# First feed-forward stage of a two-block transformer kernel: its first two weight chunks read the residual times the norm weight, and the root is applied to their banks

## The reference, cut to what matters

```
h = x
h = h + 0.5 * _swiglu(_rmsnorm(h, ffn1_norm[i]), ffn1_w_in[i], ffn1_w_out[i])
```

## Time and profile before

| | us |
|---|---|
| median of 3 runs | 1517.85 (1516.86 to 1518.26) |
| span of the profiled execution | 1515.1 |
| median less span | 2.75 |
| PE busy in that span | 1482.7 (98%) |
| DVE busy | 1177.7 (78%) |
| ACT busy | 819.8 (54%) |

### The profile page before, as it was taken

The page is one execution under the profiler, slowest core; times in us unless marked ns, Lnnn a source line. Parts: engine busy times, 40 slices in busy tenths (PEclk is TensorE's granted clock), DMA queues, the critical chain, the costliest instruction groups (busy, mean ns, idle before and its releaser), DMA issues.

```text
span 1515.1 us, 22326 instructions
## 1 busy us (share of the span) xinstructions
PE 1482.7 (98%) x9258; PEld 1317.9 (87%) x9258; DVE 1177.7 (78%) x1394; ACT 819.8 (54%) x998; POOL 49.6 (3%) x40
## 2 busy tenths in 40 slices
PE   8999999899999999999999899999999999999998
PEld 6888889898888988888888888889888889988886
DVE  6988989689889778889667798888866566786654
ACT  6645354575553575444577665455645445565442
POOL 1000015200000000000000000000000000000000
PEclk9999999999999999999999999999999999999999
DMA  8988955279889559889534398897555555465551
GB/s 286 310 290 285 340 190 167 84 253 309 297 281 324 178 192 305 291 284 310 163 112 142 131 302 291 284 327 247 189 187 181 182 166 168 141 220 179 185 183 66
DMA packets 275972, 341.69 MB, mean 226 GB/s; under 512 B 6931, under 2 KB 256939, under 8 KB 275872
## 3 DMA queue, kind: packets, MB, share of 16 engines
q1 hardware_dynamic: 273904, 334.74, 66.8%
q0 software_dynamic: 1968, 5.54, 1.1%
HBM read 339.18 MB, written 2.63 MB: 226 GB/s over the span
## 4 chain that ended last, share of the span: by engine, by line
PE 87%; DVE 7%; ACT 4%; issue 1%; DMA 1%; DVEq 0%; SPq 0%; ACTq 0%
PE banks L1688 43%; PE banks L1689 22%; PE banks L1620 5%; PE banks L1622 5%; PE banks L1621 5%; DVE w_lo L990 1%; ACT w_hi L533 1%; DVE xn L1061 1%; DVE ada_acc L1108 1%; ACT xs L563 1%; DVE x_res L1134 1%; PE banks L1760 1%; ACT xn L552 1%; DVE xs L1009 1%; DMA ada<-in_ada_w 1%
## 5 line engine op out<-in xcount | busy, mean ns | idle before, releaser
L1688 PE MATMUL banks<-xs,w_hi 128*128 128x512 f32 x1952 | 687.4, 396 | 3.6 <-DVE w_lo L990 3.6
L990 DVE TENSOR_TENSOR w_lo<-raw,w_hi 128x2048 fp32r<-128x2048 f32 (+1 forms) x241 | 538.1, 2237 | 169.3 <-ACT w_hi L533 169.0
L533 ACT ACTIVATE w_hi<-raw 128x2048 fp32r<-128x2048 f32 (+1 forms) x249 | 464.3, 1868 | 217.7 <-PE banks L1689 182.8
L1689 PE MATMUL banks<-xs,w_lo 128*128 128x256 f32 x1952 | 547.9, 281 | 0.0
L1688 PEld LDWEIGHTS banks<-xs,w_hi 128*128 128x128 f32 x1952 | 368.4, 189 | 92.1 <-DVE w_lo L990 4.8
L1688 PE MATMUL banks<-g_pair,w_hi 128*128 128x512 f32 x1056 | 370.4, 393 | 0.0
L1689 PEld LDWEIGHTS banks<-xs,w_lo 128*128 128x128 f32 x1952 | 368.8, 189 | 0.0
L1689 PE MATMUL banks<-g_pair,w_lo 128*128 128x256 f32 x1056 | 294.7, 279 | 0.0
L1688 PEld LDWEIGHTS banks<-g_pair,w_hi 128*128 128x128 f32 x1056 | 197.9, 187 | 47.1
L1689 PEld LDWEIGHTS banks<-g_pair,w_lo 128*128 128x128 f32 x1056 | 197.9, 187 | 0.0
L1108 DVE SCALAR_TENSOR_TENSOR ada_acc<-ada,c_act,ada_acc 128x1152 f32<-128x1152 f32 x124 | 175.3, 1414 | 9.3 <-DMA ada<-in_ada_w 6.5
(11 more groups left out here) (302 smaller groups left out, 1696.0 us busy)
## 6 DMA issues: line engine op xcount, KB each, us to landing
ada<-in_ada_w SPq DMA_DIRECT2D x128, 576.0 KB, 6.5
raw<-in_ffn_wg SPq DMA_DIRECT2D x44, 1024.0 KB, 5.4
raw<-in_ffn_wu SPq DMA_DIRECT2D x44, 1024.0 KB, 5.4
raw<-in_ffn_w_in SPq DMA_DIRECT2D x43, 1024.0 KB, 6.3
raw<-in_ffn_wd SPq DMA_DIRECT2D x32, 1024.0 KB, 5.2
raw<-in_ffn_w_out SPq DMA_DIRECT2D x16, 1024.0 KB, 5.2
raw<-in_ffn_wd SPq DMA_DIRECT2D x16, 768.0 KB, 4.6
raw<-in_attn_w_qkv SPq DMA_DIRECT2D x12, 1024.0 KB, 5.3
```

Of the source, the lines that this page charges most:

```text
L533: act.activation(w_hi[:, s, 0:width(c)], raw[:, s, 0:width(c)], ACT.Copy).then_inc(hi_ready, 1)
L990: dve.tensor_tensor(w_lo[:, s, 0:width(c)], raw[:, s, 0:width(c)], w_hi[:, s, 0:width(c)].bitcast(F32), ALU.subtract).then_inc(lo_ready, 1)
L1688: pe.matmul(o, wh[:, k, m], pair, start=first, stop=False, skip_group_check=True)
L1689: return pe.matmul(o[:, 0:T], wl[:, k, m], pair[:, 0, :], start=False, stop=last, skip_group_check=True)
```

## The change

Stage 0 joins the deferred stages: `DEFER` becomes `(0, 2, 7, 9, 11)`. ACT's eight squares go to GpSimd, in front of its DMA of the constants `consts`. ACT and DVE make the parts of x times weight as x arrives. SP first loads the eight columns of the norm weight alone, then a part of x and a quarter of chunk 0 in turn, then chunk 1, the other columns, chunk 2. PE runs ten 128-column matmuls on constants ahead of everything, chunk 0 and chunk 1 by `wide_u`, the sums of squares between them. The two small matmuls for the attention constants move behind chunk 1, and the constants on DVE and ACT move behind the split of chunk 4.

```
-DEFER = (2, 7, 9, 11)
+WARM = 10
+DEFER = (0, 2, 7, 9, 11)
...
                 if c == 0:
+                    sp.dma_start(cols[:, 0:KT], a["cols"][:, 0:KT]).then_inc(gain_in, 16)
                     for g in range(4):
+                        k = slice(2 * g, 2 * g + 2)
+                        sp.dma_start(x[:, k, :], a["x"][:, k, :]).then_inc(x_in[g], 16)
                         sp.dma_start(quarter(g, raw).rearrange("p (k n) -> p k n", k=2), src[:, 2 * g:2 * g + 2, :])\
...
+            pool.wait_ge(memsets, 9)
+            for k in range(KT):
+                pool.wait_ge(x_in[k * X_PARTS // KT], 16)
+                pool.tensor_tensor(xn[:, k, :], x[:, k, :], x[:, k, :], ALU.mult).then_inc(sq_ready, 1)
             pool.dma_start(consts[:, :, :], a["consts"]).then_inc(consts_in, 16)
...
+                    if n == 0:
+                        for g in range(4):
+                            u_high(0, d, 2 * g)
+                            u_high(0, d, 2 * g + 1)
+                            first_high(g)
+                        second_high(0)
+                        second_high(1)
+                        split(BASE[d] + 2)
+                        split(BASE[d] + 3)
...
                 if n == 0:
+                    for g in range(4):
+                        u_low(0, 2 * g)
+                        u_low(0, 2 * g + 1)
+                        first_low(g)
                     for b in range(3):
                         add_squares(0, b)
...
+                    second_low(0)
+                    second_low(1)
...
+                    if n == 0 and a == 2:
+                        constants()
...
+                    if a == 2 and n == 0:
+                        attention_constants()
...
             pe.wait_ge(memsets, 9)
+            for _ in range(WARM):
+                pe.matmul(bank[0][:, 0:P], ones_d[:, :], ones_c[:, :], start=True, stop=True, skip_group_check=True)
```

More of the change, by code:

```diff
@@ L543, in square @@
             def square(n, k):
[L544 to L547, removed]
+                act.wait_ge(x_ready, 8 * (n - 1) + k + 1)
                 if n + 1 < len(STAGES) and JOINT[n + 1]:
@@ L670, in ffn @@
                     ins.then_inc(silu_done, 1)
+                    if n == 0:
+                        act.activation(c_act[:, :], cols[:, COLS["c_2"][0]:COLS["c_2"][0] + ADA_T], ACT.Silu)\
+                            .then_inc(ev("c_act"), 1)
                 else:
@@ L674, in ffn, with constants @@
                     act.activation(two(silu_g), sides(0)[0], ACT.Silu).then_inc(silu_done, 1)
[L675 to L677 removed]
                     split(c0 + 3)
[L679 to L688 removed]
+                def constants():
+                    act.wait_ge(ev("lam_sum"), 1)
+                    act.wait_ge(ev("rows_copied"), 1)
+                    act.activation(lam_e[:, :], bank[1][:, SKEW:SKEW + 2], ACT.Exp).then_inc(ev("lam_exp"), 1)
+                    at = COLS["final_norm"][0]
+                    act.activation(joint_g[:, :], cols[:, at:at + 2 * KT], ACT.Square).then_inc(ev("joint_sq"), 1)
+                    act.wait_ge(ev("joint_sq"), 1)
+                    act.activation(joint_g[:, :], joint_g[:, :], ACT.Sqrt, bias=eps_col[:, :])\
+                        .then_inc(ev("joint_g"), 1)
+                    act.wait_ge(ev("joint_g"), 1)
                 for a in range(2, GATED + 1):
@@ L1656, in wide_u @@
                         pe.wait_ge(xhi_ready, SPLIT_AT[n] + k + 1)
+                    if n == 0 and first and k % 2 == 0:
+                        pe.wait_ge(first_lo, k // 2 + 1)
+                    if n == 0 and not first and k % 4 == 0:
+                        pe.wait_ge(lo_ready if k else second_lo, 1)
                     for o, m in halves:
@@ L1689, in joined, with wide_joined @@
                 return pe.matmul(o[:, 0:T], wl[:, k, m], pair[:, 0, :], start=False, stop=last, skip_group_check=True)
-            def wide_joined(s, at, n, each, halves=False):
-                order = [(k, nb) for k in range(KT) for nb in range(2)] if each or halves else \
+            def wide_joined(s, at, n, each):
+                order = [(k, nb) for k in range(KT) for nb in range(2)] if each else \
                     [(k, nb) for nb in range(2) for k in range(KT)]
                 for k, nb in order:
-                    if halves and nb == 0 and k % 4 == 0:
-                        pe.wait_ge(lo_ready if k else second_lo, 1)
                     if each and nb == 0:
```

80 lines of the change are left out of this document (27 added, 53 removed).

## The result

The changed kernel takes 1521.78 us in the median of eight runs (1519.53 to 1523.46), the kernel before 1517.88 beside it: a ratio of 1.0027 (95% interval 1.0018 to 1.0036). A second series, of the same kernel against 1517.98, gave 1519.94 us and 1.0014 (1.0005 to 1.0023). So the change makes the kernel **slower, by 2 to 4 us**, where 0.1 us was forecast. The profiled execution of the changed kernel has a span of 1520.9 us in a run of 1523.05, so it lies above its own median.

What follows compares the result with a forecast made beforehand. PE, busy 98% of 1515.1 us, was taken as the bound, held by the root and the constants: 22.7 + 22.1 puts chunk 5 at 44.8 against 44.69, so 1517.85 + 0.1 = 1518.0 us; range 1515.4 to 1521.0.

Steps and rivals of the forecast that it cites:

- The mark: First matmul of chunk 5 on PE, at 44.69 us before; a start edit is worth what it moves this.
- The chain behind U: U 2.73 us after ACT's split of chunk 3 begins; PE starts chunk 3 at U + 9.82, chunk 5 at U + 22.1.
- U: DVE's first scaling of the first bank, after ACT's root; forecast at 22.7 us (21.8 to 23.7).
- The landing of chunk 3: Chunk 3's load, which ACT's split waits for, forecast in between 19.1 and 21.0 us; 20.0 taken.
- packets of the last engine: Estimated allowance in chunk 3's landing: these may end up to 0.8 us later.
- The time outside the span: Run time beyond the profiled span, up to the median of 1517.85 us; claimed to stay at 2.75 us.
- The range: Forecast time of 1515.4 to 1521.0 us, leaving out some 0.07 below and 0.09 above.
- Warm matmuls, early chunk 0, squares, consts hidden: Start of the first feed-forward: PE's early work, GpSimd's squares and the consts load claimed covered by the wait for U.
- The rule on the shared port: DVE beside GpSimd's squares: by the rule, early low parts up to 4.6 us later, the sum some 1.7 us worse.
- Late squares: Rival: long GpSimd code reload delays the squares, chunk 5 2.7 to 5.6 us late, 1520.5 to 1523.4 us; chance 0.12.
- An open start: Rival: chunk 3 lands at 18.6 and the constants hide, chunk 5 2.3 us earlier, 1515.5 us; chance 0.14.
- the change does not do what it says: Rival: loads land no earlier, chunk 0 starts at 12.5 at slow pace, chunk 5 2.2 us late, 1520.1; chance 0.06.

Runs made afterwards that it cites:

- x first: Changed kernel with four loads of x, then four of chunk 0, instead of alternating them; ratio 1.0021 to the kernel before.
- the first trace: First profiled execution of the changed kernel, with nothing edited; its series measured 1521.78 us, ratio 1.0027 to the kernel before.
- the last version: Changed kernel with root before chunk 3's split, consts and other columns behind chunk 3, attention constants after chunk 6, DVE splitting chunk 3 before second-bank scaling; 1515.07 us, 0.9985.
- chunk 4 held: Changed kernel with the load queue waiting for chunk 3 to land before issuing chunk 4 and three ada loads; ratio 1.0018 to the kernel before.

## Why the prediction was wrong, point by point

- **The mark.** Right. Over thirteen traces chunk 5 goes from 41.87 to 48.80, and the ratios follow: 2.8 us early is 0.9985, 0.5 late 1.0003, 2.5 late 1.0016 to 1.0018. "x first" (1.3 late, 1.0021) lies outside its interval; one trace gives chunk 5 of one execution, and its profiled run was the fastest of ten.
- **The chain behind U** (2.73, 9.82, 22.1). Right to 0.03 us in the three traces of the changed kernel, read from stage 2 and the old constants. The constants cost 0.96 of PE's time where 1.0 was said.
- **The landing of chunk 3. This step failed.** The consts did go out beside it (issued at 12.46), and the byte sum of the earlier trace rows with them (19.8, and 0.4 for the new load) gave the landing of the first part (measured 19.92 to 20.12 in all variants with the same bytes). Then the prediction allowed at most 0.8 us for "packets of the last engine", an estimate that no row carried, and took the middle of a range that has the consts both out of the way and in it. Measured: the last part is 1.0 to 2.0 us behind the first where the packet of instructions adds nothing, 2.4 to 3.1 where it does. So the landing was 21.15 to 23.07 instead of 20.0, and chunk 5 1.3 to 3.3 us late instead of 0.1. The kernel before could not show it in this place: its chunk 3 went into an empty queue, with a spread of 0.46. But chunks 1 and 2 there have 0.94 and 0.85, and the first load after the packet of instructions a lone part 1.4 late; I read the DMA view by rate alone, not by what released the waiting engine.
- **The time outside the span.** It was held fixed at 2.75 us, and the changed kernel's is some 0.4 us longer than that of the kernel before. With chunk 5 at 1.3 to 3.3 late this makes 1.7 to 3.7 us; the two series measured 2.0 and 3.9.
- **The range.** 21.0 as the upper end of the landing shut out every trace of the changed kernel. The upper time, 1521.0, came from another rival; the first series lies above it, the second inside.
- **Warm matmuls, early chunk 0, squares, consts hidden.** Right for the first three, in PE's and DVE's time; the 0.4 us above come with the squares. The wait for the consts ahead of chunk 2 is hidden too; their bytes are not: they cost the landing 0.9 us, where the prediction had 1.2 and counted half.
- **The rule on the shared port** (Trainium skill, SBUF — State Buffer, section Who interferes with whom). It has the second of the two wait for the whole of the first. The traces agree that they stretch each other, a low part from 0.68 to 1.10 and a square from 0.59 to 0.88 (3.51 for four). It did not cost 4.6 us but 0.6 at the issue of chunk 3, and nothing that shows at its landing.
- **Late squares.** Out: GpSimd's first square began at 4.88, 1.51 us after its last instruction and put down to x's load. The 6 us that the Trainium skill gives for a first call (GPSIMD Engine Reference, section Instruction dispatch) are not seen in this place.
- **An open start** and **the change does not do what it says.** Both out: chunk 0 starts at 7.91, in the first trace at the fast pace, yet chunk 5 is late. The first needed the edits of the last version.

## What to carry to other kernels

A load counts as landed when the slowest of its sixteen parts is in: in a queue that never runs dry, add the spread of parts that earlier loads show in the trace (here 1 to 2 us, with a long packet in the way up to 3) to what the bytes say. Put what needs no load ahead of what waits for one: with the root ahead of the split U came at 23.10, behind it at 23.93 to 25.84. Starting an engine earlier was worth nothing here, where the chain that it waits for hung on a load of its own.

## What was unexpected of the hardware

- One packet of 16 KB of instructions takes 1.0 to 1.5 us, and in eight of fourteen traces one of a load's sixteen parts then lands 1.0 to 1.6 us behind the others. With TensorE started earlier it came at 20 instead of 25.5, onto the load that mattered.
- The parts of a load lag by what the loads ahead of it lagged (0.9 to 2.1 us, trace by trace), as long as the queue does not run dry. What sets the lag stays open.
- With nothing queued behind it, chunk 3's last recorded packet ended at 21.44 and its landing came at 22.39 (chunk 4 held).
- TensorE ran at the lower level at the idle stretches of 3.46 and 4.96 us, and at the one of 2.23 us in some traces of a kernel and not in others (850 us: 0.51 or 1.00). From chunk 5 to the end the traces take 1469.7 to 1472.9 us, as far apart as the change itself.
- Ten warm matmuls, the same in each trace, left chunk 0 at the fast pace in six of eleven traces and at the slow one in five.
